# Norm chains and residual sums per token tile in a two-block fp32 kernel, with a lead of two transposed pairs ahead of three products

## The reference

```
h = h + rms_norm(mixed @ w_out) * g_post          # residual sum
f = rms_norm(h) * g_pre                            # rows of the next product
next = f @ w_next
```

## Time and profile before

| what | value |
|---|---|
| median of 3 runs | 1858.09 us (1856.0 to 1858.85) |
| the profiled execution's own time | 1857.85 us |
| its span in the trace | 1856.4 us |
| TensorE matmuls, busy | 1825.0 us, 98% of the span |
| TensorE weight loads, busy | 1581.7 us, 85% |
| VectorE, busy | 1463.7 us, 79% |
| ScalarE, busy | 899.9 us, 48% |
| DMA, mean rate | 230 GB/s |
| mean granted TensorE clock | 0.997 |

### The profile page before, as it was taken

How to read it: one execution, slowest core, us unless ns; L and a number is a source line. 1 busy time by engine, 2 the same in 40 slices (tenths; PEclk the granted TensorE clock), 3 DMA queues, 4 the chain that set the end, 5 groups by cost and what they waited for, 6 DMA issues and landing times. The chain is left out here.

```text
span 1856.4 us, 26725 instructions
## 1 busy us (share of the span) xinstructions
PE 1825.0 (98%) x10206; PEld 1581.7 (85%) x10206; DVE 1463.7 (79%) x1687; ACT 899.9 (48%) x1160; POOL 112.6 (6%) x217
## 2 busy tenths in 40 slices
PE   8999999999999999999999999999999999999997
PEld 8999978888888888888888878888888888888886
DVE  5799987777888897889887877755788677887854
ACT  6434566454434443543344557423556545445452
POOL 0000000100000000000000000000111010001000
PEclk9999999999999999999999999999999999999999
DMA  8755446868787786778967946653655783868662
GB/s 323 243 185 187 147 157 233 300 200 283 242 289 243 260 272 228 233 251 303 267 221 261 315 172 221 226 182 136 226 194 214 259 295 127 280 217 282 205 227 91
DMA packets 190473, 426.95 MB, mean 230 GB/s; under 512 B 12448, under 2 KB 12832, under 8 KB 188704
## 3 DMA queue, kind: packets, MB, share of 16 engines
q1 hardware_dynamic: 162144, 323.75, 51.1%
q0 software_dynamic: 27648, 100.68, 16.3%
q10 hardware_dynamic: 576, 1.05, 0.2%
HBM read 421.23 MB, written 4.21 MB: 229 GB/s over the span
## 5 line engine op out<-in xcount | busy, mean ns | idle before, releaser
L536 ACT ACTIVATE w_hi<-raw 128x1024 fp32r<-128x1024 f32 x552 | 580.3, 1058 | 689.1 <-PE banks L1957 340.4
L1092 DVE TENSOR_TENSOR w_lo<-raw,w_hi 128x1024 fp32r<-128x1024 f32 x552 | 668.1, 1222 | 250.9 <-ACT w_hi L536 248.5
L1932 PE MATMUL banks<-a_pair,w_hi 128*128 128x512 f32 x1536 | 541.4, 398 | 0.2 <-issue 0.2
L1934 PE MATMUL banks<-a_pair,w_lo 128*128 128x256 f32 x1536 | 430.0, 280 | 0.0
L1932 PEld LDWEIGHTS banks<-a_pair,w_hi 128*128 128x128 f32 x1536 | 288.6, 188 | 70.0 <-issue 0.4
L1955 PE MATMUL banks<-w_hi,b_hi 128*128 128x512 f32 x808 | 317.1, 392 | 0.7 <-DVE w_lo L1092 0.7
L1956 PE MATMUL banks<-w_lo,b_hi 128*128 128x512 f32 x808 | 314.7, 390 | 0.0
L1957 PE MATMUL banks<-w_hi,b_lo 128*128 128x512 f32 x808 | 314.7, 390 | 0.0
L1131 DVE SCALAR_TENSOR_TENSOR mod_sum<-mod_raw,silu_c,mod_sum 128x1024 f32<-128x1024 f32 x240 | 303.1, 1285 | 12.4 <-DMA mod_raw<-in_ev_mod_w 9.8
L1934 PEld LDWEIGHTS banks<-a_pair,w_lo 128*128 128x128 f32 x1536 | 289.9, 189 | 0.1
L1920 PE MATMUL banks<-a_pair,w_hi 128*128 128x256 f32 x768 | 221.4, 288 | 0.4 <-ACT scratch L923 0.4
(11 more groups left out here) (228 smaller groups left out, 1690.4 us busy)
## 6 DMA issues: line engine op xcount, KB each, us to landing
raw<-in_w_ff SPq DMA_DIRECT2D x128, 1024.0 KB, 6.5
mod_raw<-in_ev_mod_w POOLq DMA_DIRECT2D x96, 512.0 KB, 5.3
mod_raw<-in_od_mod_w POOLq DMA_DIRECT2D x96, 512.0 KB, 5.2
raw<-in_ev_w_in SPq DMA_DIRECT2D x40, 1024.0 KB, 5.2
raw<-in_w_in SPq DMA_DIRECT2D x39, 1024.0 KB, 5.1
raw<-in_od_w_in SPq DMA_DIRECT2D x32, 1024.0 KB, 6.7
raw<-in_w_out SPq DMA_DIRECT2D x16, 1024.0 KB, 5.2
raw<-in_ev_w_out SPq DMA_DIRECT2D x16, 1024.0 KB, 6.7
```

What stands on the lines that cost most here:

```text
L536: nc.scalar.activation(w_hi[:, s % SLOTS], raw[:, s // 2, KPS * (s % 2):KPS * (s % 2) + KPS, :], ACT.Copy).then_inc(hi_ready, 1)
L1092: nc.vector.tensor_tensor(w_lo[:, s % SLOTS], raw[:, s // 2, KPS * (s % 2):KPS * (s % 2) + KPS, :], w_hi[:, s % SLOTS].bitcast(F32), ALU.s ...
L1932: nc.tensor.matmul(out[:, f, :], wh, rows[:, :, k, :], start=s == 0 and t == 0, stop=False, skip_group_check=True)
L1934: last = nc.tensor.matmul(out[:, f, T:2 * T], wl, rows[:, 0, k, :], start=False, stop=s == STEPS - 1 and t == KPS - 1, skip_group_check=True)
```

## The change

All sums and roots that were made for both token tiles at once are made for each tile. Semaphores `head_cols` and `h_ready` become one for each tile, and `transposes` takes the token tile as its outer loop and waits for each tile's diagonal and each tile's part of h. The numbers of expected roots are written in tables VAR and STD.

```diff
-WARM = {0: 13, 1: 14, 2: 20, 4: 22}
+WARM = {0: 13, 1: 9, 2: 17, 4: 15}
...
-            sp.wait_ge(h_ready, 16)
+            for tt in range(TT):
+                sp.wait_ge(h_ready[tt], 2 * NBLK)
             sp.dma_start(tok(h_dram), X).then_inc(h_out, 16)
             sp.dma_start(Y, tok(io["ctx"])).then_inc(x_in, 16)
```

ScalarE's roots take the last column's sum as input, the rest as bias, and stand behind each tile's squares:

```diff
+            def post_root(name, tt):
+                act.wait_ge(var_ready, VAR[name])
+                nc.scalar.activation(norm_s[:, 4 + tt:5 + tt], ssq_part[:, tt, NBLK - 1:NBLK], ACT.Sqrt, bias=post_base[:, tt:tt + 1],
+                                     scale=1.0 / D).then_inc(std_ready, 1)
+            def residual_root(name, tt):
+                act.wait_ge(var_ready, VAR[name] + tt)
+                nc.scalar.activation(norm_s[:, 4 + tt:5 + tt], sums[:, 3, tt:tt + 1], ACT.Sqrt, bias=sums[:, 4, tt:tt + 1],
+                                     scale=1.0 / D).then_inc(std_ready, 1)
...
+            residual_root("evq", 1)
             split_hi(b + 1, [2])
-            root(4)
-            split_hi(b + 1, [3])
             def first_pairs(m, block, scale, shift):
                 first_column(m, scale, shift, a_hi)
-                pair_modulated(m, scale, shift, a_hi, range(1, 4))
+                pair_modulated(m, scale, shift, a_hi, [1])
+                split_hi(block, [3])
+                pair_modulated(m, scale, shift, a_hi, [2, 3])
                 split_hi(block, [4])
```

In place m = 1 ScalarE's order behind its roots is as before. On VectorE, the sums of the first three column blocks are made ahead of the last tile's work, and the residual adds of tile 0 before tile 1's sums are there:

```diff
+            def post_sums():
+                link(nc.vector.tensor_reduce(norm_s[:, 0:2], ssq_part[:, :, 0:NBLK - 1], AX.X, ALU.add))
+                nc.vector.tensor_scalar(post_base[:], norm_s[:, 0:2], 1.0 / D, RMS_EPS, ALU.mult, ALU.add).then_inc(var_ready, 1)
+            def post_scale(name, tt):
+                dve.wait_ge(std_ready, STD[name] + tt)
+                link(nc.vector.reciprocal(resid_s[:, tt:tt + 1], norm_s[:, 4 + tt:5 + tt]))
+            def residual_square(name, tt, squares):
+                r = resid_s[:, tt:tt + 1]
+                dve.wait_ge(std_ready, STD[name] + tt)
+                nc.vector.reciprocal(r, norm_s[:, 4 + tt:5 + tt])
+                dve.wait_ge(xy_done, squares)
+                link(nc.vector.tensor_scalar(norm_s[:, 2 + tt:3 + tt], xy_part[:, tt, NBLK - 1:NBLK], sums[:, 2, tt:tt + 1], None, ALU.add))
+                dve.wait_ge(yy_done, squares)
+                link(nc.vector.tensor_scalar(norm_s[:, tt:tt + 1], yy_part[:, tt, NBLK - 1:NBLK], sums[:, 1, tt:tt + 1], r,
+                                             ALU.add, ALU.mult))
+                nc.vector.tensor_scalar(sums[:, 3, tt:tt + 1], norm_s[:, tt:tt + 1], norm_s[:, 2 + tt:3 + tt], r,
+                                        ALU.add, ALU.mult).then_inc(var_ready, 1)
```

In place m = 1:

```diff
-            post_scale(1, lambda: gained(6, 3, out_acc[3], None, [1]))
+            gained(6, 3, out_acc[3], None, [0])
+            post_scale("out", 0)
             dve.wait_ge(x_in, 16)
+            head_residual(0, 0)
+            head_residual(1, 0)
+            add_to_residual([1], [0])
+            gained(6, 3, out_acc[3], None, [1])
             dve.wait_ge(acc_free, 2 + ACC["ff"])
-            add_to_residual(range(2))
+            post_scale("out", 1)
+            head_residual(0, 1)
+            head_residual(1, 1)
+            add_to_residual([1], [1])
```

In place m = 2 (in place m = 4 tile 0's second head add stands before `last_tile(1)`):

```diff
-            post_scale(3, lambda: last_tile(1))
-            residual_sums(4, TT * NBLK)
+            residual_square("ff", 0, TT * NBLK - 1)
+            head_residual(0, 0)
+            last_tile(1)
+            residual_square("ff", 1, TT * NBLK)
+            head_residual(0, 1)
+            residual_scale("evq")
+            head_residual(1, 0)
+            head_residual(1, 1)
```

In `first_pairs` on VectorE, for m = 2 and 4:

```diff
                 first_pair(m, scale, shift, a_hi, a_lo)
                 add_to_residual([1])
-                add_to_residual([2])
                 pairs(1)
                 split_lo(block, [2])
-                add_to_residual([3])
+                add_to_residual([2])
                 pairs(2)
                 split_lo(block, [3])
                 pairs(3)
                 split_lo(block, [4])
+                add_to_residual([3])
                 pairs(4)
...
                 split_lo(block, [7])
+                link(nc.vector.tensor_tensor(sums[:, 0, :], sums[:, 0, :], sums[:, 3, :], ALU.add))
+                residual_base()
```

The lead, the end of the program and the gate vector:

```diff
-            norm_product(1, BLOCK["ff"], ACC["ff"], wide_step, 3)
+            norm_product(1, BLOCK["ff"], ACC["ff"], wide_step, 2)
...
-                    norm_product(2, BLOCK["evq"], ACC["evq"], step_tokens, 3)
+                    norm_product(2, BLOCK["evq"], ACC["evq"], step_tokens, 2)
...
-            norm_product(4, BLOCK["odu"], ACC["odu"], wide_step, 3)
+            norm_product(4, BLOCK["odu"], ACC["odu"], wide_step, 2)
...
-            post_scale(8, lambda: gained(2 * (3 * NBLK - 1), NBLK - 1, acc[1], None, [1]))
+            gained(2 * (3 * NBLK - 1), NBLK - 1, acc[1], None, [0])
+            post_scale("odo", 0)
+            add_to_residual(range(3), [0])
+            gained(2 * (3 * NBLK - 1), NBLK - 1, acc[1], None, [1])
             dve.wait_ge(acc_free, 2 + ACC["odo"] + 4)
-            add_to_residual()
+            post_scale("odo", 1)
+            add_to_residual([0], [1])
+            add_to_residual([3], [0])
+            add_to_residual(range(1, NBLK), [1])
...
-            gate_steps = [(1, 0, 1, 0), (1, 1, 1, 0), (1, 0, 1, 0), (1, 0, 1, 0), (0, 0, 0, 1), (1, 1, 1, 1), (1, 1, 1, 1), (2, 2, 0, 0)]
+            gate_steps = [(1, 0, 1, 0), (1, 1, 1, 0), (1, 0, 1, 0), (1, 0, 1, 0), (0, 0, 0, 1), (1, 1, 1, 1), (1, 1, 2, 1), (1, 2, 0, 0)]
...
-                    if n == 7 and m == 2:
-                        mod_turn("od_gate", 0, 0, 4, raw_temp)
+                    if n == 7 and m >= 2:
+                        turn_parts("od_gate", 0, 0, 4, raw_temp, 2 * (m - 2), 2)
```

More of the change, by code:

```diff
@@ L255, in build_program @@
         raw_first = sem("raw_first")
-        head_cols = sem("head_cols")
+        head_cols = [sem(f"head_cols{i}") for i in range(TT)]
         pair_tmp = sem("pair_tmp")
@@ L268, in build_program @@
         std_ready = sem("std_ready")
-        h_ready = sem("h_ready")
+        h_ready = [sem(f"h_ready{i}") for i in range(TT)]
         scale_ready = sem("scale_ready")
@@ L759, in out_block @@
                                          accum_out=ssq_part[:, tt, i:i + 1]).then_inc(y_squared, 1)
+                    if i == 3:
+                        act.wait_ge(y_squared, TT * i + tt + 1)
+                        post_root("out", tt)
             load_root()
@@ L773, in _ @@
                 residual_squares([c])
-            root(2)
+            root("ffn")
             split_hi(b + 4, [4])
@@ L882, in _ @@
             split_hi(b + 1, range(2))
-            root(5)
+            root("ctx")
             split_hi(b + 1, range(2, 4))
@@ L1070, in _ @@
                     split_hi(b + 1, range(4))
-                row_block("odo", n, n % 2, range(TT), 4 if n == 3 else 0)
-            root(8)
+                for tt in range(TT):
+                    row_block("odo", n, n % 2, [tt], 4 if n == 3 else 0)
+                    if n == NBLK - 1:
+                        act.wait_ge(y_squared, TT * (2 * NBLK + n) + tt + 1)
+                        post_root("odo", tt)
             for c in range(NBLK):
                 part = slice(BW * c, BW * (c + 1))
-                act.wait_ge(h_ready, TT * (3 * NBLK + c) + 2)
+                act.wait_ge(h_ready[1], 3 * NBLK + c + 1)
                 nc.scalar.dma_start(out[P:2 * P, part], X[:, 1, part]).then_inc(out_done, 16)
@@ L1410, in gained @@
                         e.then_inc(each_tile, 1)
-                if not each_tile and TT - 1 in tiles:
-                    e.then_inc(acc_free, 1)
+                if not each_tile:
+                    if TT - 1 in tiles:
+                        e.then_inc(acc_free, 1)
+                    else:
+                        link(e)
             dve.wait_ge(grow_in, 16)
@@ L1456, in gained_products, with products_before @@
                         dve.wait_ge(xy_done, xy_count[0] - TT)
-                    nc.vector.scalar_tensor_tensor(xy_junk[:, tt, :], Y[:, tt, part], 1.0, X[:, tt, part], ALU.mult, ALU.mult,
+                    nc.vector.scalar_tensor_tensor(xy_junk[:, tt, :], Y[:, tt, part], 2.0, X[:, tt, part], ALU.mult, ALU.mult,
                                                    accum_out=xy_part[:, tt, i:i + 1]).then_inc(xy_done, 1)
-            def residual_sums(n, squares):
+            def products_before(squares):
@@ L1462, in residual_sums @@
                 dve.wait_ge(yy_done, squares)
                 dve.wait_ge(xy_done, squares)
-                xx, yy, xy, t, base = (sums[:, i, :] for i in range(5))
-                nc.vector.tensor_reduce(yy, yy_part[:], AX.X, ALU.add)
-                link(nc.vector.tensor_reduce(xy, xy_part[:], AX.X, ALU.add))
-                link(nc.vector.tensor_tensor(t, yy, resid_s[:], ALU.mult))
```

(12 more changed lines are left out.)

105 lines of the change are left out of this document (54 added, 51 removed).

## The result

The changed kernel took 1865.41 us (median of 6 runs, 1860.89 to 1867.85) against 1859.44 for the kernel before in the same comparison: ratio 1.0031, 95% interval 1.002 to 1.0043. So it is slower, by 5.8 us on the 1859 of before, where 2.15 slower was forecast; the time lies outside the range. All ratios here leave out two executions in a slower state, one of 6871 us (kernel before) and one of 2590 us (three pairs with early splits), which the medians still hold.

What follows compares the result with a forecast made beforehand. TensorE, busy 98% of the span, was taken to bound the kernel. +2.45 (A) + 3.0 (B) + 0.1 (C) - 2.05 (D) - 1.2 (gate) - 0.15 (start) = +2.15 on 1857.85: 1860.2 us, range 1856.0 to 1863.5.

Steps and rivals of the forecast that it cites:

- A: From w_out to feed-forward: first step 0.9 us earlier, but waits for low splits make it +2.45 us in all.
- P0: First of a product's eight steps, P0 to P7; forecast earlier by 0.9, 3.2 and 3.6 us at A, B and C.
- P6: Seventh of a product's eight steps; forecast to wait for the low split, 2.8 us at A, about 0.7 at B.
- B: Feed-forward to the attention layer's first product: later last add delays the context load, so Q comes 3.0 us later.
- Q: First step of the next product; at B forecast at 1126.2, +3.0 us, after TensorE stands idle 4 us.
- P7: Last of a product's eight steps; at B forecast to wait about 0.9 us for the low split.
- C: Attention layer to pooling layer: P0 3.6 us earlier, eaten up by the queues behind pair 7; +0.1 us.
- D: The kernel's end: three blocks of tile 0 added and written before tile 1's root is known; -2.05 us.
- The gate: Gate vector, for which the pool product waited 1.4 us: its sum comes 1.2 us earlier; -1.2 us.
- The start: First product of the kernel: one diagonal less to wait for; -0.15 us.
- Rival 1: At B, TensorE's clock falls to half after the 4 us hole, losing 2 to 4 us: 1863.3 us; chance 0.17.

Runs made afterwards that it cites:

- three pairs with early splits: Changed kernel with three pairs of transposes ahead of P0 and, at B, the next weight block's splits ahead of the context squares: 1858.71 us, ratio 0.9984.
- second measurement: The changed kernel timed again with no edit, for the spread and a second profile: 1864.49 us, ratio 1.0028.
- Two pairs alone: Kernel before with only two pairs of transposes, not three, ahead of P0 at A, B and C: 1866.81 us, ratio 1.0033.
- The late add alone: Kernel before with only the last residual add at B and C moved behind the split of step 4, from behind that of step 2: 1859.43 us, ratio 0.9998.
- three pairs and the early add: Changed kernel, three pairs ahead of P0, last residual add at B and C ahead of pair 2: 1852.91 us, ratio 0.9965; again 1854.30 us, ratio 0.997.
- old-end run: Changed kernel with both tiles' gain products and reciprocals before all eight adds at the end, as in the kernel before: 1865.55 us, ratio 1.0027.

## Why the prediction was wrong

Each place is measured from the last weight load ahead of it, which leaves out what happened earlier; "before" is its one profile.

- **A, +2.45.** P0 came 0.9 to 1.2 earlier (load to P0 6.08 before, 5.21 and 4.91 after), P6's hole was 2.94 for 2.8, P6 came 2.3 to 2.6 later. Right.
- **B, +3.0.** Load to P0 fell by 2.6 (3.2 forecast), since the first transposes came 0.4 earlier and not 1.05. Q came 3.3 later (38.39, then 41.64 and 41.66). Landing took 12.8 for 13.1. The mechanism is right, holes at P6 and P7 too (0.67 and 1.08 for 0.7 and 0.9), the size 0.3 short.
- **C, +0.1.** P0 came 3.1 earlier for 3.6, so Q came 0.6 later (37.92, then 38.55 and 38.52), just outside the bound of 0.5.
- **D, -2.05.** It gave -1.8. The gate: its wait went from 1.4 to 0.2, so -1.2. The start: A is reached 0.2 and 0.3 earlier in the two profiles, with the falls near 262 set aside, for -0.15.
- **The sum** of the stages is so +3.0 to +3.3, where +2.15 was forecast: about 1 us is mis-sized, at B, C and D.
- **The clock** is the step that failed. At A it was not priced at all, though the prediction works out a hole of 2.8 us there; it fell in all six profiles that have this hole unfilled. At B the prediction gave the fall 0.17, "against it: the hole is hardly longer than 3.6"; it fell in all six profiles with a hole of 2.7 to 3.8 there, and in none of the five with 1.4 to 2.0. Two falls of 1.71 are 3.4 us, and 3.0 to 3.3 with 3.4 is 6.4 to 6.7: the measured 5.8, with an interval of 3.7 to 8.0 by the ratios, agrees (5.2 in the second measurement, 3.2 to 7.3).

Behind that stands a reading error. "The trace's one fall came after TensorE's last matmul" was false: the kernel before has one at 262, behind an attention step's hole of 2.9 us. The granted clock of the kernel before is 0.83 in 260-270 us; that sets the price of a fall (1.71) and makes A's hole suspect. Rival 1 was the right mechanism with half its places. Its price was too high: half clock "for about as long as the hole", 2 to 4 us, comes from no row, and the runs show 3.4 us at half clock behind holes of 2.94 and 3.77 us alike, so 1.71. With A's fall added the rival would have been 1863.3 + 1.7 = 1865.0; that this is so near the measured 1865.4 is luck, one term too high against others too low.

Which part is to blame is settled by the single parts. Two pairs alone cost 6 to 7 us. The late add alone costs nothing that can be timed in the kernel before, and 3 to 4 us in the changed kernel. The split end gives 1.8. Without the two costly parts the rest of the change is a gain of some 6 us (three pairs and the early add).

## What to carry to other kernels

Price a hole in TensorE's stream of about the size that had falls here (2.7 us and more) at its length plus the clock's fall behind it, and take that price from the granted clock over the whole trace of before, not from the stretch under study. Fewer transposes ahead of a product move the first step forward and the last ones back: what is queued behind the last pair on the other engines decides, and these queues must be reordered with it. And ask of each moved instruction what hangs on it on a DMA queue: the late add held up a spill, and behind it the context and the next weights.

## What the runs showed beside

**A fall can be a matter of chance at the same hole.** The hole near 259 to 261.6 us (2.8 to 2.9 us) is the same in every kernel here. Of 14 profiles with it unfilled the clock fell behind it in 7, in the 2 with it filled in none. A short hole is no safeguard either: near P0 of C the clock fell in two of the four profiles with three pairs and the tile-wise sums, where the longest gap between weight loads is 1.92 us in all four. All falls ahead of the last product but the double one at B of the old-end run cost 1.71 us.

**Wide products run at one of two paces.** In the pooling layer, with nothing waiting and the clock at 1.00, the same matmuls come at 346.7 or 353.3 ns a pair (a product of 512 columns and one of 256), from the first to the last. The weight loads of line 2001 between 1600 and 1700 us, first profile of the changed kernel:

```profile
L2001 PEld LDWEIGHTS banks<-a_pair,w_hi x289: 187/187/188, 1600.0 to 1699.9; 128*128 128x128 f32 x145
```

and its second profile:

```profile
L2001 PEld LDWEIGHTS banks<-a_pair,w_hi x284: 187/188/188, 1599.9 to 1699.9; 128*128 128x128 f32 x142
```

289 against 284 of them in one stretch: over the layer's some 500 pairs that is 3 us. The feed-forward's first group has the two paces also (1.7 us), its other three ran at 353.3 in every profile. The kernel before had the quick pace in the pooling layer in its profile. What sets the pace is open. With the falls and the waits for weights near 900 us (0.4 to 2.6 us in sum), it makes the runs of one kernel differ by 5 to 8 us, so a difference of 2 us is better read stage by stage than from the times.
